# Chunks of a normed input 2064 bytes apart in place of 2048, tiles for the down products 2080 bytes apart

## What is computed

```python
n = rms_norm(h, attn_norm);  z = n @ w_in              # then gated linear attention and latent attention
h = h + concat([o_g, o_m]) @ w_out
m = rms_norm(h, mlp_norm)
h = h + square(relu(m @ w_mlp_up)) @ w_mlp_down        # 1024 -> 4096 -> 1024
gate = sigmoid(rms_norm(h, ple_norm) @ w_ple_gate + b)
h = h + (p @ w_ple_proj) * gate
# second block, twice: a mixer (pooling, then chunk attention), and
h = rmsnorm(x, ffn_norm)
x = x + (silu(causal_dwconv3(h @ w_gate)) * (h @ w_val)) @ w_out      # 1024 -> 2816 -> 1024
```

## The kernel before

| tile | before | modulo 256 | step between chunks | after |
|---|---|---|---|---|
| AH | 37,632 | 0 | 2048 | 37,632, step 2064 |
| AL | 54,016 | 0 | 2048 | 54,144, step 2064 |
| WH0, WL0 | 86,784 and 111,360 | 0 | (unit dependent) | 256 bytes further |
| HH0 | 149,568 | 64 | 2048 | 149,824, step 2080 |
| HL0 | 170,048 | 64 | 2048 | 170,624, step 2080 |
| pH | 198,784 | 128 | 2048 | 199,680 |

## Time and profile before

### The profile page before, as it was taken

One profiled execution on the slowest core, in us unless ns is written; L12 is line 12 of the kernel. 1 busy time (PEld: TensorE's weight loads), 2 busy tenths in 40 slices (PEclk: granted clock), 3 DMA queues, 4 the chain that ended last, 5 costly groups with the idle time before them and its releaser, 6 DMA issues.

```text
span 1644.3 us, 19097 instructions
## 1 busy us (share of the span) xinstructions
PE 1638.7 (100%) x8084; PEld 1336.2 (81%) x8084; DVE 939.2 (57%) x1385; ACT 615.9 (37%) x828; POOL 84.6 (5%) x80
## 2 busy tenths in 40 slices
PE   9999999999999999999999999999999999999999
PEld 7877878888888888888888888877777888888887
DVE  6797665444333547577466457555655576366353
ACT  5576344322332346433222223355565333122121
POOL 1300000000000000000000000311201100000000
PEclk9999999999999999999999999999999999999999
DMA  5310227454454421223322223323221223222311
GB/s 187 116 36 27 103 93 128 120 89 130 87 111 85 135 88 52 77 103 107 124 83 96 103 83 100 123 78 101 77 76 52 77 103 104 102 102 94 110 59 71
DMA packets 28054, 155.94 MB, mean 95 GB/s; under 512 B 3712, under 2 KB 5392, under 8 KB 12096
## 3 DMA queue, kind: packets, MB, share of 16 engines
q1 hardware_dynamic: 26352, 149.75, 25.6%
q0 software_dynamic: 1328, 4.86, 5.0%
q10 hardware_dynamic: 288, 0.10, 0.0%
HBM read 149.98 MB, written 4.72 MB: 94 GB/s over the span
## 4 chain that ended last, share of the span: by engine, by line
PE 98%; ACT 1%; DVE 1%; POOL 0%; DMA 0%; issue 0%; SPq 0%; DVEq 0%
PE bank L585 26%; PE bank L587 26%; PE bank L586 26%; PE bank L591 3%; PE bank L593 3%; PE bank L592 3%; PE bank L1216 1%; PE bank L840 1%; PE bank L1226 1%; PE bank L1242 1%; PE bank L825 1%; PE bank L865 1%; PE bank L850 1%; PE bank L769 0%; PE bank L1102 0%; PE bank L1204 0%
## 5 line engine op out<-in xcount | busy, mean ns | idle before, releaser
L585 PE MATMUL bank<-AH,WH 128*128 128x512 f32 (+1 forms) x1150 | 451.4, 393 | 0.2 <-DVE X L1707 0.2
L587 PE MATMUL bank<-AH,WL 128*128 128x512 f32 (+1 forms) x1150 | 447.8, 389 | 0.0
L586 PE MATMUL bank<-AL,WH 128*128 128x512 f32 (+1 forms) x1150 | 447.6, 389 | 0.0
L1677 DVE TENSOR_TENSOR WL<-RAW,WH 128x2048 fp32r<-128x2048 f32 (+1 forms) x133 | 298.5, 2247 | 190.7 <-ACT WH L1287 190.7
L1287 ACT ACTIVATE WH<-RAW 128x2048 fp32r<-128x2048 f32 (+1 forms) x133 | 248.3, 1871 | 260.1 <-PE bank L587 240.3
L585 PEld LDWEIGHTS bank<-AH,WH 128*128 128x128 f32 (+1 forms) x1150 | 215.5, 187 | 48.0 <-issue 2.6
L587 PEld LDWEIGHTS bank<-AH,WL 128*128 128x128 f32 (+1 forms) x1150 | 215.5, 187 | 45.8
L586 PEld LDWEIGHTS bank<-AL,WH 128*128 128x128 f32 (+1 forms) x1150 | 215.6, 187 | 45.6 <-issue 1.0
L585 PE MATMUL bank<-HH,WH 128*128 128x512 f32 x608 | 239.6, 394 | 0.0
L587 PE MATMUL bank<-HH,WL 128*128 128x512 f32 x608 | 238.4, 392 | 0.0
L586 PE MATMUL bank<-HL,WH 128*128 128x512 f32 x608 | 236.0, 388 | 0.0
(11 more groups left out here) (306 smaller groups left out, 1732.9 us busy)
## 6 DMA issues: line engine op xcount, KB each, us to landing
RAW<-in_W SPq DMA_DIRECT2D x124, 1024.0 KB, 4.8
RAW<-in_W SPq DMA_DIRECT2D x9, 768.0 KB, 4.1
X<-in_XT SPq DMA_DIRECT2D x16, 256.0 KB, 5.5
ev_scratch<-ev POOLq DMA_DIRECT2D x16, 160.0 KB, 7.5
Gb<-ev_scratch SPq DMA_DIRECT2D x16, 128.0 KB, 2.9
Gb<-ev_scratch SPq DMA_DIRECT2D x16, 112.0 KB, 2.7
out<-X SPq DMA_DIRECT2D x7, 256.0 KB, 2.0
RAW<-in_W SPq DMA_DIRECT2D x2, 512.0 KB, 5.4
```

The lines of the kernel that those rows point to most:

```text
L585: e.matmul(o, a, h, start=first, stop=False)
L586: e.matmul(o, a, l, start=False, stop=False)
L587: return e.matmul(o, c, h, start=False, stop=last)
L1677: e.tensor_tensor(k.WL[j][:, 0:n], k.RAW[RAW_OF[u]][:, 0:n], k.WH[j][:, 0:n].bitcast(F), SUB).then_inc(*WLO.mark(u))
```

## The change

Four allocations get a longer row of which the same 512 values are used, and one address formula follows:

```diff
     k.X = a.tile("X", [P, 8, S])
-    k.AH = a.tile("AH", [P, 8, S], R)
+    k.AH = a.tile("AH", [P, 8, S + 4], R)[:, :, 0:S]
     al_at = a.at
-    k.AL = a.tile("AL", [P, 8, S], R)
+    k.AL = a.tile("AL", [P, 8, S + 4], R)[:, :, 0:S]
...
     a.at = base
-    k.HH = [a.tile(f"HH{i}", [P, S], R) for i in range(NH)]
-    k.HL = [a.tile(f"HL{i}", [P, S], R) for i in range(NH)]
+    k.HH = [a.tile(f"HH{i}", [P, S + 8], R)[:, 0:S] for i in range(NH)]
+    k.HL = [a.tile(f"HL{i}", [P, S + 8], R)[:, 0:S] for i in range(NH)]
...
     k.band = [a.over(f"band{i}", [P, 4, BW], at) for i, at in
-              enumerate([base + 4 * S * 8] + [base + 4 * S * (NH + 8) + 4 * 4 * BW * i for i in range(3)])]
+              enumerate([base + 4 * (S + 8) * 8] + [base + 4 * (S + 8) * (NH + 8) + 4 * 4 * BW * i for i in range(3)])]
```

## The result

The changed kernel takes 1672.24 us (median of 4 runs, 1670.69 to 1673.72) against 1647.13 us before: ratio 1.0153, 95% interval 1.0138 to 1.0167. It is 25.1 us, or 1.5%, **slower**. The forecast was 1634.0 us, faster, with a range up to 1660 us; both were wrong. Rival B, a good case that the change breaks, is what happened, at a price between its two figures of 1655 and 1678 us.

A forecast was written before the change was run, and what follows sets the result against it. The prediction took PE to bound the kernel through the distance between matmul starts. A third of 39.5 us (23.1 for AH/AL, 16.4 for HH/HL), 13.2 us, came off 1647.2, giving 1634.0 us; range 1604 to 1660 us.

The forecast's parts named there:

- Rival B: AH's regular beat was the good case and the change breaks it: 1655 us, or 1678 at 233.3 ns; chance 0.34.
- What bounds the kernel: Whole kernel: PE busy 1638.7 of 1644.3 us, waits under 3 us; time is matmul count times start-to-start distance.
- The 2.9 us around the span: Median of the runs 1647.2 us against the profiled span of 1644.3 us; carried over unchanged.
- The address has a price: AH and HH stretches of equal work differ by about 2 ns per matmul (226.9 against 229.0) by operand place.
- I take a third of the first end: AH/AL and HH/HL matmuls: a third of the upper gain of 39.5 us, so 13.2 us less.
- remainder of 13.4 ns: AH's 512-column distance beyond the 213.3 ns stream, read as instruction-change cost rounded up to whole 6.67 ns beats.
- I cost them at nothing: The 672 matmuls with AH or AL as weights, lines 591 to 593, were expected to change by nothing.
- The bounds: AH/AL and HH/HL matmuls: at most 39.5 us gained at 220.0 ns, at most 31 us lost at 233.3 ns.
- Rival A: Places modulo 64 do not matter and the remainder is a fixed instruction-change cost: 1647 us, within 0.2%; chance 0.14.

The follow-up runs named there:

- the stream alone: Kernels issuing only 96 float32r matmuls per case, no other engine working, none of the reference's outputs computed; 226.7 ns per matmul with moving operand and weights at multiples of 256.
- weights64: The kernel before with all weight tiles and what lies behind them moved up 64 bytes, AH, AL, HH and HL at their old places modulo 256; 1665.06 us, ratio 1.0111.

## Why the prediction was wrong

- **What bounds the kernel**: right. PE is all of the time, the time is count times distance, the waits stay under 3 us in all. The loss is in the distance alone. The 2.9 us around the span were a mix of two things: in every run whose span is on record beside its time the time is 1.7 to 2.0 us above it, and the remaining 1 us is probably the fall of the clock, which the profiled execution did not have and the three runs, by their times of 1647.0 to 1647.3 us, had. It does not bear on the difference.
- **"The address has a price"**: right, and the size of HH's (2.3 ns) was confirmed by taking it away.
- **The step that failed** is "I take a third of the first end, because one step of three changes its place in the 64-byte beat". It rested on the inference that the remainder of 13.4 ns is a rounding to places modulo 64, which a shift would relieve. The rows already spoke against it: AH and HH both lie at multiples of 64 bytes, and they differed by 2 ns. The runs show in its place a difference modulo 256 between moving operand and weights, for which the kernel before had the best value, 0, in AH. Leaving it costs 5 ns at once: 16.3 us lost in place of 7.7 us gained (a third of 23.1) for AH. HH lay at an unchanging 64, and the changing places cost it 3 ns more: 6.3 us lost in place of 5.5 gained.
- The evidence for the failed step was three column counts whose distances were multiples of 6.67 ns. Those of 480 and 496 columns (216.7 and 223.3 ns), which the kernel does not use, are not. Three points on one ruler were too few.
- **"I cost them at nothing"** for the 672 matmuls with AH as weights: wrong by 2.4 us. The weights' place counts as the moving operand's does. I had looked only at whether the weight tiles keep their place.
- **The bounds**: 31 us of loss at 233.3 ns held as an upper end, and the result lies inside it (25.1), but with some luck: the rows did not bound the unseen places, and 4 bytes off gives 238.0 ns in the stream alone. I then cut the range at 1660, because I gave rival B the price of HH's present distance. With every row of 512 columns off a multiple of 256 slower than the ones on it, the price of the unseen should have been taken between 229.0 and 233.3: with the middle, 4.2 x 3450 + 2.2 x 1824 = 18.5 us, 1666 us, and with more chance than the forecast.
- **Rival B** had the mechanism right in kind: a good case broken, and distances that no longer repeat with the chunk. They do repeat with the product of 8 chunks, so "never settles" goes too far. Its reason (AL 128 bytes further against the weights) is a part only: with AL at AH's place the stream takes 232.0 just the same.
- **Rival A** is refuted by the result, 1672.2 us where it has 1647, and by the stream alone, where the moving operand 16 bytes off costs 5 ns. The prediction had named two statements of the Trainium skill for it, in "SBUF — State Buffer": lines of 16 bytes ("Specifications (TRN2)"), and a TensorE that waits on nobody ("Who interferes with whom"). That a shift by a multiple of 16 bytes changes nothing was my conclusion from them, and the measurement decides against it: in `weights64` the weights 64 bytes further cost 1.23 us in every AH stretch. That TensorE waits on no other engine is not touched: the stream alone shows the same distances with no other engine at work. The 215.8 ns that follow from the formula of the Trainium skill in "TensorE: Matmul & The Clock Gate", "Wait — 56ns, not 53.3ns?", were reached by none of the 57 cases with 512 adjacent moving columns in these float32r streams; the best is 226.7.

## What to carry to other kernels

Where float32r matmuls of 512 moving and 128 weight columns follow each other, put the moving operand and the weights at the same place modulo 256 bytes, and make the steps between chunks a multiple of 256: padding that is meant to spread addresses cost 5 ns a matmul here. For other shapes try the places first, since with 256 columns another place was the best. Two stretches of the same work with different speed in one trace are a hint at the layout, and the direction to go is towards the faster one, not to a third place that no row has seen. And when an engine is full, look at the distance between starts; the busy share is 100% in all these kernels, from 1641 to 1672 us.

## What the runs showed that I had not expected

- As long as the places do not change from matmul to matmul, only the difference between the two operands' places counts: both 64 bytes off is as good as both at 0 (226.7 ns), one alone 64 off costs 2.2 or 6.7 ns by its sign.
- The moving operand 4 bytes off is worse than 64 off: 238.0 against 228.9 ns.
- The 24 distances of a product repeat in the changed kernel, product by product: the distance follows the addresses even where it looks like noise.
- The clock can fall to half for some matmuls in one execution and not in another of the same order of work, worth about 1.3 us, more than some of the differences sought here.
- Fewer weight columns do not help: 32 columns 231.7 ns, 128 columns 226.7.
- A moving operand taken from every second element takes 453.3 ns, twice the time of an adjacent one.
- The remainder over the stream alone (0.417 ns a column) stays at 13.3 ns or more wherever 512 columns were tried; 256 columns come down to 6.7 at a difference of 192 bytes. Why it is there at all is open.
